# Input projection by pairs of tiles: seven block products per column half in place of eight

## The reference, cut to what matters

```python
for l in range(DEPTH):                                  # DEPTH = 2
    h = rms_norm(x, norm_mix[l])                        # x: (1, 2048, 1024)
    proj = jnp.einsum('bsd,de->bse', h, w_in[l])        # w_in[l]: (1024, 2048)
    q_a, k_a, v_a, u_b, q_c, k_c, v_c, g_c = jnp.split(proj, IN_SPLITS, axis=-1)
    y_a = sliding_window_sink_attention(q_a, k_a, v_a, ...)
    y_b = multiscale_pool(u_b, ...)
    y_c = retention(q_c, k_c, v_c, g_c, pos)
    x = x + jnp.einsum('bse,ed->bsd', concat(y_a, y_b, y_c), w_out[l])
    x = x + moe_ffn(rms_norm(x, norm_ffn[l]), ...)      # router, top 2 of 32 experts
```

## Time and profile before

| what | value |
|---|---|
| median of 3 runs | 3203.95 us (3203.49 to 3205.53) |
| profiled execution: span, first to last instruction | 3202.4 us |
| profiled execution's own time | not listed apart; the runs around it are 1.1 to 3.1 us above the span |
| PE busy / weight loads | 3135.7 us (98%) / 2327.6 us (73%) |
| DVE / ACT / POOL busy | 1410.7 (44%) / 614.9 (19%) / 1079.4 us (34%) |
| mixer, layer 1 / layer 2 (first projection to first expert product, on PE) | from 11.38 to 850.10 us / from 1614.85 us |
| first half of the output projection with the ranks behind it (PE, 388.69 to 395.92) / second half (to 402.87) | 7.23 / 6.95 us |
| granted TensorE clock, mean | 0.998 |
| DMA, mixer slices / expert slices | mostly 1 to 3 tenths busy / 8 to 9 tenths |

### The profile page before, as it was taken

The page is one execution under the profiler, slowest core; times in us unless marked ns, Lnnn a source line. Parts: engine busy times, 40 slices in busy tenths (PEclk is TensorE's granted clock), DMA queues, the critical chain, the costliest instruction groups (busy, mean ns, idle before and its releaser), DMA issues.

```text
span 3202.4 us, 56050 instructions
## 1 busy us (share of the span) xinstructions
PE 3135.7 (98%) x19076; PEld 2327.6 (73%) x19076; DVE 1410.7 (44%) x4344; ACT 614.9 (19%) x1742; POOL 1079.4 (34%) x1250
## 2 busy tenths in 40 slices
PE   8999999999899999999999999999998999999998
PEld 5565565655699999988765555655656999998887
DVE  2666766767422222111136767667664222222111
ACT  4222222222201111111142222222222111111011
POOL 1322313223255555433122313223132555554222
PEclk9999999999999999999999999999999999999999
DMA  8123122220689899999942131231217899899996
GB/s 298 57 73 85 45 86 60 70 86 30 229 284 305 306 313 300 350 351 349 326 157 86 44 86 51 80 85 45 86 32 266 282 307 303 293 326 340 358 344 222
DMA packets 223996, 623.99 MB, mean 195 GB/s; under 512 B 65328, under 2 KB 118576, under 8 KB 190128
## 3 DMA queue, kind: packets, MB, share of 16 engines
q1 hardware_dynamic: 177584, 542.53, 47.2%
q0 software_dynamic: 46112, 77.70, 10.4%
HBM read 542.46 MB, written 78.78 MB: 194 GB/s over the span
## 4 chain that ended last, share of the span: by engine, by line
PE 91%; DMA 3%; DVE 2%; issue 2%; ACT 1%; SPq 1%; DVEq 1%; POOL 1%; POOLq 0%; ACTq 0%
PE bank L1691 30%; PE bank L1442 19%; PE bank L1476 13%; PE bank L1731 9%; PE bank L1721 6%; PE bank L1433 3%; PE bank L1436 3%; PE bank L1395 2%; PE bank L1548 1%; PE bank L1597 1%; PE bank L1625 1%; DMA wts<-in_w_in 1%; DMA arena<-out 1%; PE bank L1487 1%; PE bank L1561 0%
## 5 line engine op out<-in xcount | busy, mean ns | idle before, releaser
L1691 PE MATMUL bank<-arena,wts 128*128 128x128 f32 (+7 forms) x8192 | 1005.5, 283 | 21.4 <-issue 17.4
L1691 PEld LDWEIGHTS bank<-arena,wts 128*128 128x128 f32 x8192 | 990.3, 191 | 46.7 <-issue 43.0
L1442 PE MATMUL bank<-wts,arena 128*128 128x512 f32 x1536 | 691.4, 597 | 5.2 <-DVEq L1000 2.7
L1442 PEld LDWEIGHTS bank<-wts,arena 128*128 128x128 f32 x1536 | 280.2, 190 | 306.5 <-issue 298.0
L1476 PE MATMUL bank<-wts,arena 128*128 128x512 f32 x1024 | 453.6, 595 | 1.6 <-ACT arena L873 1.6
L1372 DVE TENSOR_TENSOR arena<-arena,bank 128x128 f32<-128x128 f32 (+6 forms) x64 | 19.1, 299 | 941.1 <-ACT arena L930 941.1
L1476 PEld LDWEIGHTS bank<-wts,arena 128*128 128x128 f32 x1024 | 191.5, 190 | 229.5 <-issue 212.8
L697 POOL DMA_INDIRECT arena<-hrows,arena x288 | 292.1, 1014 | 167.7 <-issue 152.5
L594 POOL TENSOR_TENSOR arena<-arena 128x256 f32<-128x256 f32 x32 | 23.1, 721 | 831.9 <-DVEq L1111 831.9
L722 POOL DMA_INDIRECT out<-arena x176 | 275.2, 1564 | 55.4 <-issue 54.3
L1731 PE MATMUL bank<-arena,wts 128*128 128x135 f32 (+6 forms) x2176 | 280.1, 289 | 0.0
(11 more groups left out here) (226 smaller groups left out, 3122.9 us busy)
## 6 DMA issues: line engine op xcount, KB each, us to landing
wts<-in_w_gate SPq DMA_DIRECT2D x128, 1024.0 KB
wts<-in_w_up SPq DMA_DIRECT2D x128, 1024.0 KB
wts<-in_w_down SPq DMA_DIRECT2D x128, 1024.0 KB
arena<-out SPq DMA_DIRECT2D x176, 128.0 KB, 3.0
hrows<-arena SPq DMA_DIRECT2D x38, 512.0 KB, 3.7
out<-arena SPq DMA_DIRECT2D x36, 512.0 KB, 14.5
arena<-in_x SPq DMA_DIRECT2D x32, 512.0 KB, 7.2
arena<-out SPq DMA_DIRECT2D x32, 512.0 KB, 7.1
```

What stands on the lines that cost most here:

```text
L1442: i = mm(bIP[n % 2][:, :], hT[:, d], win[:, n, d], start=(d == 0), stop=(d == DC - 1))
L1691: return mm(gu_at(f, k, w), lhs, xT[:, d, 0:w], start=start, stop=(d == DC - 1), skip_group_check=True)
```

## The change

Tiles 0 to 2 and tile 15 are still projected whole, one chunk of 512 columns at a time (`whole`). Tiles 3 to 14 are projected by pairs (t, t+1). In steps 2 to 13 PE makes one half (1024 columns) of one pair per step. Seen as blocks, that is [2 tiles x 2 halves of the 1024 inner elements] times [2 halves x 2 chunks of 512 columns]: eight block products of 4 matmuls each. The new code makes seven (`factor`), as in Strassen's and Winograd's scheme: three take blocks as they are, four take sums of blocks of the weights (`make`, on DVE, 8 blocks per layer, stored to the DRAM tensor `wt`) and sums of blocks of the tiles (four additions per pair on POOL), and the outputs are put together in PSUM (accumulating on what is there), by ACT copies (`partial_columns`) and by three DVE additions per step (`finish_columns`). Products have the signs and factors of the scheme; what is computed is the same up to rounding.

What comes with it:
- The weights are no longer resident from step 2 on. A ring of four slots of 1 MB (`ring`, 128 x 2048 f32) is filled by SP with one block per product, from w_in or from `wt`; the place of chunks 2 and 3 of w_in is used for other tiles.
- The tile's norm is applied before the transpose: ACT makes four sums of squares of the pieces `xq`, PE adds them over groups of rows (`sumsq`), DVE runs the Newton iteration on four columns, multiplies by row factor and gain (four instructions), and transposes (`hT_of`). The second load of x (`xf`), the scaling of w_in, `norm_front` and the product for u's row factor go.
- This runs three tiles ahead: step s prepares tile s+3. Step 0 projects tiles 0 and 1, step 1 tile 2, steps 2 to 13 the pairs, steps 14 and 15 tile 15.
- u is projected like the rest and transposed by PE (`u_turn`, two transposes).
- The norms of q and k of tile s (`qk_sums`, `qk_scaled`) move to the front of DVE's step.

The core of the diff:

```diff
+                    def factor(j):
+                        first, second = pair_of(s)
+                        k = (s - 2) * 7 + j
+                        pair = (first - 1) // 2
+                        if j == 0:
+                            e.wait_ge(hT_ready, l * TILES + second + 1)
+                            e.wait_ge(x_new, (t0 - 2) * 2 + 1)
+                        if j == 1:
+                            e.wait_ge(x_new, (t0 - 2) * 2 + 2)
+                        if j == 2:
+                            e.wait_ge(sums_ready, l * 6 + pair)
+                            e.wait_ge(act_out, act_of(l, s, 0))
+                        if j == 3:
+                            e.wait_ge(dve_out, dve_of(l, s, 0))
+                        if j == 4:
+                            e.wait_ge(act_out, act_of(l, s, 1))
...
+                        e.wait_ge(ring_full[k % SLOTS], slot_full(l, k))
+                        top, low = by_d(blocks_12[pair % 2]), by_d(blocks_22[pair % 2])
+                        own = (top[:, 0:4], top[:, 4:8], sums_of[1], sums_of[2], sums_of[0], sums_of[3], low)[j]
+                        for d in range(4):
+                            i = mm(bIP[j in (1, 3, 6)][:, :], own[:, d], ring[k % SLOTS][:, d], start=(d == 0 and j in (0, 1, 3)),
+                                   stop=(d == 3), skip_group_check=True)
+                        i.then_inc(prod_done, 1)
...
+                    def hT_of(t):                                  # DVE
+                    e.wait_ge(pe_sumsq, l * TILES + t + 1)
+                    rstd(rfq, bB[:, 256:260], D)
+                    for g in range(4):
+                        piece_of = xq[:, PIECE * g:PIECE * g + PIECE]
+                        v.scalar_tensor_tensor(out=piece_of, in0=piece_of, scalar=rfq[:, g:g + 1], in1=gmix, op0=ALU.mult, op1=ALU.mult)
...
+                def finish_columns(s, i):                          # DVE
+                    n = 2 * (s % 2)
+                    t, u = pair_of(s)
+                    to = (columns(t, n), columns(u, n + 1), columns(u, n))[i]
+                    e.wait_ge(act_out, act_of(l, s, (0, 2, 1)[i]))
+                    e.wait_ge(prod_done, prod_of(l, s, (1, 3, 6)[i]))
+                    v.tensor_tensor(to, to, bIP1[:, :], ALU.add).then_inc(dve_out, 1)
...
+                def partial_columns(s, i):                         # ACT
+                    e.wait_ge(prod_done, prod_of(l, s, (0, 2, 4, 5)[i]))
+                    a((columns(t, n), columns(u, n), columns(u, n + 1), columns(t, n + 1))[i], bIP0[:, :], ACT.Copy).then_inc(act_out, 1)
...
+                    if s % 2 and s < 12:                           # POOL
+                        ahead = (s + 1) // 2 % 2
+                        wait_alone(e, hT_ready, t0 + 4)
+                        wait_alone(e, prod_done, whole_prod(l, 2, 3) if s == 1 else prod_of(l, s, 5))
+                        first, second = by_d(blocks_12[ahead]), by_d(blocks_22[ahead])
+                        e.tensor_tensor(sums_of[0], by_d(block_21), second, ALU.add)
+                        e.drain()
+                        e.tensor_tensor(sums_of[1], sums_of[0], first[:, 0:4], ALU.subtract)
+                        e.tensor_tensor(sums_of[2], first[:, 0:4], by_d(block_21), ALU.subtract)
+                        e.drain()
+                        e.tensor_tensor(sums_of[3], first[:, 4:8], sums_of[1], ALU.subtract)
+                        e.drain().then_inc(sums_ready, 1)
...
+                    if s in FACTORED:                              # SP
+                        for j in range(7):
+                            wait_alone(e, prod_done, prod_of(l, s, j))
+                            load_block((s - 2) * 7 + j + SLOTS)
```

540 lines of the change are left out of this document (370 added, 170 removed).

## The result

The changed kernel takes 3306.6 us (median of 4 runs, 3303.4 to 3309.7) against 3204.5 us (4 runs) on the same chip: a ratio of 1.0322, 95% interval 1.0309 to 1.0335. The forecast was 3234 us, at most 3276. The sign was right, the size was not: +102 us in place of +30.

What follows compares the result with a forecast made beforehand. PE, busy 98%, was taken as the bound, with DVE and ACT chains making it wait after the change. Layer starts +65, steps 14 and 15 -23, steps 2 to 13 -12: +30 us, 3234 us; range 3192 to 3276.

Steps and rivals of the forecast that it cites:

- the second wait: Output projection, steps 2 to 13: PE waits 1.5 us for DVE's `ycT_ready` copy, done at 39.0 + w.
- w: PE's wait at a step's fifth product, for ACT's copy behind the exponentials: 1.1 us, bounds 0.3 and 4.
- the term of 0.3 us a step for POOL's additions: End of odd steps: POOL's four new additions beside DVE's work, counted as 0.3 us a step on the mean.
- contended DVE: DVE instructions at the end of odd steps each wait out a POOL addition: 2 us or more, 3258 us; chance 0.12.
- PE alone: Steps 2 to 13 without either forecast wait: 46.5 us a step, as a rival 3164 us; chance 0.14.
- First wait: Fifth product of steps 2 to 13: PE waits for ACT's copy behind the exponentials, 1.1 us, bounds 0.3 and 4.
- Third wait: `rank_read` before the next step's transposes: held to be no wait, DVE's places done at 47.7 + w, next step at 48.0 + w.
- The clock: PE's lower clock level after idling: 1.7 us counted at the start of a layer, nothing for steps 2 to 13.
- Steps 14 and 15: Mixer's late steps, set by DVE alone: 44.9 and 38.0 us, -11.3 a layer, -23 in all.
- Start of a layer: Before step 2, one more tile projected and normed before its transpose: +28.7 in layer 1, +36.7 in layer 2, together +65.
- about 4 us late (0 to 12): Layer 1's start: tile 4's pieces delayed in SP's queue by stores of made blocks and 5 MB of padding, about 4 us.
- the rival that had said 3306 us: Steps 2 to 13: products wait for ring blocks, or blocks delay the pieces, 3 us more a step; 3306 us, chance 0.10.

Runs made afterwards that it cites:

- the fastest kernel: Changed kernel with joint Newton, late sums of squares, ACT's `ycT_ready` copy, earlier fifth-product block and third-product copy, later tile-4 sums and padding: 0.9937 against the kernel before.
- the idle products: Changed kernel plus twenty or nine unused products before PE's `rank_read` wait at the start of steps 4, 6, 8, 10, 12: 1.0293 and 1.0322 against the kernel before.
- the joint Newton iteration: Changed kernel with tile s+3's four piece norms iterated in the same DVE instructions as the retention norms: 1.0201 against the kernel before.
- the three other edits: Changed kernel with POOL's sums behind the scatter, ACT's sums of squares behind the exponentials, and the `ycT_ready` copy by ACT: 1.0236 against the kernel before.
- the copy by ACT: Changed kernel with the `ycT_ready` copy made by ACT behind its attention-output copy, instead of by DVE behind routing: 1.0282 against the kernel before.

## Why the forecast was wrong

The step that failed is in the part on the second wait: "Behind the copy DVE has addition, `hT_of` (5.8), residual (0.6), places (1.7): done at 47.7 + w, just in time". In step 9 w was 2.16, so that means 49.9 on the step's clock, against PE's 49.8 (554.1). `rank_read` came at 52.6. DVE's rows:

```profile
544.33 0.42 DVE L1357 COPY arena<-bank 128x256 f32<-128x256 f32 x1
...
546.04 0.42 DVE L1132 TENSOR_TENSOR newton<-newton 128x4 f32<-128x4 f32 x1
546.53 0.59 DVE L1134 SCALAR_TENSOR_TENSOR newton<-newton 128x4 f32<-128x4 f32 x1
...
552.60 0.69 DVE L1241 TENSOR_TENSOR arena<-arena,bank 128x512 f32<-128x512 f32 x1 [0.28 <-issue]
```

The 2.7 us add up so: the copy ended at 40.4 (544.75, forecast 41.2), 0.7 sooner; addition and `hT_of` took 7.6 (up to 552.3) for 6.4; 0.28 us lie between the transposes and the residual; residual and places took 4.3 (from 552.60) for 2.3, and what is over is POOL's block sums beside them. Of the 1.2 us that `hT_of` took too long, 1.1 are three instructions of its Newton iteration of 0.42 to 0.59 us in place of 0.16, beside POOL's pooling sums, which the kernel before has too (POOL's L760 to L770, 545.2 to 548.0). In even steps, which have no block sums, `hT_of` is as long, and PE waits 0.55 to 0.90 us for `rank_read`. "Just in time" left no slack, so all of it became PE's.

The same fault sits in the term of 0.3 us a step for POOL's additions: leaving them out took 1.2 to 1.5 us off a step (50.3 for 51.5 to 51.8). The rival named "contended DVE" had this mechanism and named the places, and its price of 24 us in all was near the 29 to 36 us that this makes in 24 steps. I gave it a chance of 0.12, since I argued that residuals read PSUM; the places do not. Alone it would not have reached 3306 us: the other waits and the start of a layer do the rest, as follows.

Point by point, per step over 24 steps (a number of the page's groups divided by 24):

- **PE alone, 46.5.** Right within 0.4: 46.9 once nothing waits.
- **First wait, 1.1 (0.3 to 4).** 35.0 / 24 = 1.46. The pieces came at 14.8 (14.9 on the mean) and not 13.1 on the clock; the mechanism was right, as the run with the sums of squares behind the exponentials shows.
- **Second wait, 1.5.** 14.8 / 24 = 0.62. Too large: in step 9 the copy was done 0.7 sooner than forecast, and PE stood at its matmul 0.4 later (40.1, forecast 37.5 + 2.16). Moving it away showed that it hid the third.
- **Third wait, 0 (0.3 for POOL).** 35.3 / 24 = 1.47. Missed.
- **The clock.** Put at nothing in the sum for steps. 1056 instructions of L1691 at 615 ns take 18 us more than at the 598 they have in the fastest kernel; with L1757 (601 against 597) and the transposes (106.7 against 99.0 us) and the other group of L1691 (603 against 592, 288 of them), 33 us, 1.4 a step. The five terms 46.9 + 1.46 + 0.62 + 1.47 + 1.4 are the measured 51.8. But the idle products show that behind `rank_read` this last one is not a cost of its own: without it PE waits instead.

So steps 2 to 13 cost +44 us (22.7 and 21.3 in the two layers) in place of -12, and this difference of 56 is most of the 73 missed.

**Steps 14 and 15**: 46.3 and 38.6, forecast 44.9 and 38.0. DVE sets them, as said; step 14 waits 4.02 us for its transposition and 1.63 for the router's copy. Sum -19 in place of -23.

**Start of a layer**: layer 1 +34.9 (138.35 against 103.43 of the earlier trace rows), forecast +28.7; the term "about 4 us late (0 to 12)" for stores and padding was 7.7 us of wait and 3.0 of products at the lower clock behind it, and the run with the padding moved took 8.3 off (step 2 at 129.55 in place of 137.88). In layer 2, step 2 starts 110.0 us behind the first product, before 80.6: +29.4, and the first product itself is 6.9 us later, together +36.3 for a forecast of 36.7. The experts of layer 1 are unchanged (752.0 us in both kernels). Steps 16 and 17, for which the forecast had no change, take 3.3 and 3.2 us more in the two layers (in layer 1 56.9 for 53.5, from the first transposes of step 16 to the first expert product); no run took that up.

What the forecast said would show it right: the waits at the fifth product and at `ycT_ready` were there; step 2 of layer 2 at 118 us behind the layer's first pieces (forecast 117) too; DVE had, beside the wait for the retention products, 1 to 4 us of waits in steps 3 to 12; PE waited for no block but one (0.4 us in all).

## What to carry to other kernels

Where a chain of one engine is reckoned to end "just in time", it is the bound, and each small thing on it is to be priced at full, above all narrow instructions beside a working POOL. A gain on a chained wait shows in full only when the waits behind it are gone too: the joint Newton iteration gave 37 us alone and 54 on top of the three other edits (1.0236 to 1.0067). Each wait that went let the next one show: the copy by ACT raised the wait for `rank_read`, and the ring's wait came up as soon as ACT's sums were out of the way. An edit that only moves a cost along the chain gains nothing, as the one that moved POOL's sums showed. Last, an estimate that agrees with the measured total is no evidence of its mechanism: the rival that had said 3306 us was the one that its own experiment refuted.
